# One 8-wide gather ring, 512 expert picks: fewer picks handed out beside the selection of experts, more beside attention and the routing's query products

## The chip, the cores and the metric

The kernel runs on 1 core of one Trainium2 chip. The metric is the device time of one execution in microseconds; lower is better. TensorE is called PE, VectorE DVE, ScalarE ACT, GpSimd POOL and SyncE SP.

## The reference, cut to what matters

Sequence 256, width 1024, f32. A first block of two layers, each a mixer (attention) and then a feed-forward that retrieves single-neuron experts; then a second block with four kinds of attention, gates and a dense feed-forward. The part that matters here is the retrieval. Each token takes 16 experts for each of 8 heads, 128 experts in all, out of 16384:

```python
q = (xc @ w_q).reshape(t, PEER_HEADS, 2, PEER_QDIM // 2)
sc = jnp.einsum('thpc,hpnc->thpn', q, sub_keys)
v_half, i_half = lax.top_k(sc, PEER_TOPK_HALF)
cand = (v_half[:, :, 0, :, None] + v_half[:, :, 1, None, :]).reshape(t, PEER_HEADS, -1)
top_s, pos = lax.top_k(cand, PEER_TOPK)
expert = jnp.take_along_axis(cand_idx, pos, axis=-1)
g = jax.nn.softmax(top_s, axis=-1)
act = jax.nn.gelu(jnp.einsum('thkd,td->thk', u_tab[expert], xc))
return jnp.einsum('thk,thkd->td', (g * act), v_tab[expert])
```

## The kernel before

Tokens lie in two tiles of 128 (one token per partition). For each layer and tile, `route` multiplies the queries on PE (the query products, L1361, which stream 8 MB of `in_peer_w_q`), scores them against the keys (L1350), and lets DVE take the top 16 of each list and work out the 128 expert numbers (the selection, L1414 to L1490).

After that there are 128 **picks** for this layer and tile, one for each of a token's 128 experts. A pick is: POOL gathers one row for each token (L2690: u and v rows side by side, 8 KB for each of 128 partitions) into one of 8 slots of a ring (`RING`); DVE takes the dot product of u with the token (L1532); ACT applies gelu and the share (L1548, L1549); and v times the weight is added to the output, either on PE with a diagonal matrix made by ACT (L1557, L1568) or on DVE (L1540). The addition frees the slot, and POOL can gather the next row into it. POOL takes the rows strictly in order.

The picks of one layer and tile are a **feed**. Four feeds (0: layer 0 tile 0; 1: layer 0 tile 1; 2: layer 1 tile 0; 3: layer 1 tile 1) run beside the work that comes next in the program: feed 0 beside the mixer and the routing of layer 0 tile 1, feeds 1 and 2 beside the mixer and routing of layer 1, feed 3 beside the start of the second block. Where that work may be interrupted stands a **point** with a weight. Picks are handed out in proportion to the weight passed:

```python
def handed_out(f, weight):
    return f["first"] + int(weight * min((P - HELD_BACK - f["first"]) / max(f["weight"], 1.0), RATE))
```

So 122 of 128 picks are spread over the sum of a feed's weights (at most 0.6 per unit of weight), and the last 6 come in `finish_experts`. A weight is a share, not a time: raising some points takes picks from all others. At a point every engine runs its part of the same picks, in program order with its other work. Which engine adds is set in `share_out` by the kind of point: `"dve"` points (the selection's are these) have the adding done by PE, `"pe"` points (the query products) by DVE, and at `"both"` points (attention) DVE adds every third pick and PE the others. All engines run in order, so what stands behind a waiting pick waits with it. Weights for the dense products come through a second ring of 4 slots of 1 MB, loaded by SP.

Of the kernel before, what the change touches and what calls it, by code (L numbers as in the profile page):

```python
# [144 lines left out]
def build(nc, a, out):  # L145
    with ExitStack() as ctx:
# [104 lines left out]
        def handed_out(f, weight):  # L251


            return f["first"] + int(weight * min((P - HELD_BACK - f["first"]) / max(f["weight"], 1.0), RATE))

        def point(us, filled="dve"):


            f = feeds[-1] if feeds and feeds[-1]["open"] else None
            if f is None:  # L260
                return lambda name, e: None
            f["weight"] += us
            behind = f["weight"]
            f["cuts"].append(behind)
            f["filled"].append(filled)

            def run(name, e):
                at = f["cuts"].index(behind)
                for i in range(handed_out(f, f["cuts"][at - 1] if at else 0), handed_out(f, behind)):
                    f[name](e, i)  # L270
            return run
# [438 lines left out]
        def attend(groups, maps_in=scores, beside=lambda n: None, busy=None):  # L710
# [4 lines left out]
            plan = []  # L715
# [3 lines left out]
            for g in groups:  # L719
                n_out = {"joint": 1, "diff": 2}.get(g["kind"], len(g["maps"]))  # L720
                n_turned = 2 if g["kind"] == "diff" else len(g["maps"])
                chunks = g["tile"] + 1
                apart.append(beside(len(plan)))
                if plan:
                    plan[-1]["out"] = products.take()
                value = {"s": maps_in.take(), "turns": [turns.take() for _ in range(chunks)],
                         "n_out": n_out, "n_turned": n_turned, "chunks": chunks, "w": P * chunks,
                         "m": maxes_ready.plan(), "p": probs_ready.plan()}
                if g["kind"] == "stick":
                    value["m2"] = maxes_ready.plan()  # L730
                    value["a1"] = from_act.plan()
                if g["kind"] == "diff":
                    value["a2"] = from_act.plan()
                plan.append(g | value | {"points": [point(6.0, "both"), point(6.0, "both")]})
            plan[-1]["out"] = products.take()

            def sums_of(n):
# [520 lines left out]
        def hybrid(t, score_banks, angles=None):  # L1258
# [21 lines left out]
            for j in range(2):  # L1280
# [4 lines left out]
                    values=[(lambda c, i=i: values[:, c, HD + i * HD:HD + (i + 1) * HD]) for i in hs],  # L1285
                    out_ap=mixed[:, t, 512 + 256 * j:768 + 256 * j].rearrange("p (n d) -> p n d", d=HD)))
            attend(groups, score_banks, busy=None if t else hT[:, 0:4, 0:P])
            turn_wide(M, mixedT, DC, tiles)
            project(mixedT, a["hyb_w_out"], DC, D, add_residual, "dve", tiles)
# [31 lines left out]
        def route(layer, t, beside=None, halved=False):  # L1321
# [4 lines left out]
            plan, key_units = [], []  # L1326
# [10 lines left out]
            other = beside() if beside else None  # L1337
            e_in, e_out = to_act.plan(), from_act.plan()
            routed[layer, t] = [experts_ready.plan() for _ in lots]
            made = [point(7.0, "pe") for _ in range(4)] + [point(7.0, "pe")]  # L1340
            ranked = [point(us) for us in [6.0] + 5 * [3.5] + [6.0] + 6 * [4.5]]

            def pe(e):
                def score(b):
# [757 lines left out]
        def attend_second(t, banks, tmp, bias, cum, beside=lambda n: None):  # L2102
# [41 lines left out]
            if t:  # L2144

                groups.insert(3, groups.pop(1))
            attend(groups, banks, beside)

        def diff_norm_parts(t):
# [46 lines left out]
        diff_act, diff_dve, diff_point, _ = diff_norm_parts(0)  # L2196
# [43 lines left out]
        diff_act, diff_dve, _, heads_made = diff_norm_parts(1)  # L2240
        turn_pe, turn_act, turn_dve, turn_units = turn_split_parts(H, m_pair, [(0, 0), (0, 1), (1, 0), (1, 1)])
        plan = []
# [512 lines left out]
```

## Time and profile before

| | |
|---|---|
| median of 3 runs | 2141.29 us (2138.33 to 2141.95) |
| the profiled execution | 2140.08 us, its span 2138.3 us |
| busy in the span | PE 78%, DVE 70%, ACT 37%, POOL 30% |
| moved by DMA | 744.77 MB, mean 348 GB/s |
| of it by the gathers (q0) | 536.90 MB in 512 gathers |
| the chain that ended last | PE 41%, DMA 22%, DVE 19%, ACT 9% |

Stretches are named in us from the start of the span, as the trace counts them. The line with GB/s tells in which of 40 slices the DMA moved as much as it ever does here; in the slices that don't, something else set the pace. A share of busy time over the whole span says little, since stages have different limits.

### The profile page before, as it was taken

To read this page: it belongs to the slowest core of one execution; us is meant where nothing else is said; L and a number is where in the kernel's file an instruction comes from. 1 tells how busy PE (TensorE), PEld (TensorE's weight loads), DVE (VectorE), ACT (ScalarE), POOL (GpSimd) and SP (SyncE) were. 2 spreads that over 40 slices of the span, in tenths; PEclk is the share of its full clock that TensorE was granted. 3 is DMA by queue.
4 is the path that set the end of the run, shared out by engine and by line. 5 is a ranking of instruction groups with operands and counts; after the bars stand their busy time and mean duration, and the time that the engine had idled before them with its cause. 6 is when DMAs were issued, how large, how long until landed. Compare 5 with 4: busy or idle time off the path is not lost.

```text
span 2138.3 us, 20663 instructions
## 1 busy us (share of the span) xinstructions
PE 1665.0 (78%) x6490; PEld 1000.6 (47%) x6490; DVE 1493.1 (70%) x3129; ACT 788.5 (37%) x2050; POOL 648.8 (30%) x524
## 2 busy tenths in 40 slices
PE   8797777667767865877778477765767899999998
PEld 4573343622323343333344432554333375668986
DVE  5378776897766678976666897768777455566654
ACT  1213452234424422432352235212555353444432
POOL 0013454344433443543244354335454000000000
PEclk9999899889888987998889799977888999999999
DMA  7358999999999999999999999999999775574442
GB/s 277 142 221 337 404 403 421 419 416 422 419 421 392 403 421 399 412 419 421 403 368 419 392 387 421 421 422 421 376 407 403 314 307 203 199 290 158 177 178 98
DMA packets 105515, 744.77 MB, mean 348 GB/s; under 512 B 12864, under 2 KB 13504, under 8 KB 16576
## 3 DMA queue, kind: packets, MB, share of 16 engines
q0 software_dynamic: 73728, 536.90, 61.4%
q1 hardware_dynamic: 31248, 204.98, 24.5%
q10 hardware_dynamic: 432, 1.57, 0.2%
q8 instruction: 53, 0.87, 0.2%
q14 instruction: 54, 0.44, 0.1%
HBM read 742.37 MB, written 1.05 MB: 348 GB/s over the span
## 4 chain that ended last, share of the span: by engine, by line
PE 41%; DMA 22%; DVE 19%; ACT 9%; issue 6%; DVEq 1%; POOL 1%; PEldq 1%; PEld 0%; ACTq 0%; SPq 0%; POOLq 0%
DMA sb_work<-in_peer_uv,sb_expert 19%; PE ps_acc L1568 12%; PE bank L494 6%; DVE sb_x L1540 4%; DVE sb_work L1532 4%; PE bank L1361 4%; PE bank L2056 2%; DMA sb_wring<-in_peer_w_q 2%; ACT L1548 2%; PE bank L564 2%; PE bank L565 2%; PE bank L566 2%; PE ps_acc L566 2%; PE ps_acc L564 2%; PE ps_acc L565 2%
## 5 line engine op out<-in xcount | busy, mean ns | idle before, releaser
L2690 POOL DMA_INDIRECT sb_work<-in_peer_uv,sb_expert x512 | 645.8, 1261 | 1013.3 <-PE ps_acc L1568 457.5
L1568 PE MATMUL ps_acc<-sb_work,sb_diag 128*128 128x512 f32 x1304 | 689.4, 675 | 305.1 <-ACT sb_diag L1557 261.5
L1532 DVE CUSTOM_DVE_ANT_0 sb_work<-sb_work,sb_h 128x1024 f32<-128x1024 f32 x512 | 619.8, 1223 | 189.9 <-DMA sb_work<-in_peer_uv,sb_expert 183.4
L1568 PEld LDWEIGHTS ps_acc<-sb_work,sb_diag 128*128 128x128 f32 x1304 | 264.2, 215 | 674.8 <-issue 665.5
L1548 ACT ACTIVATE sb_dots<-sb_dots 128x1 f32<-128x1 f32 x512 | 102.6, 200 | 526.6 <-DVE sb_dots L1532 497.2
L1540 DVE SCALAR_TENSOR_TENSOR sb_x<-sb_work,sb_weight,sb_x 128x1024 f32<-128x1024 f32 x186 | 238.5, 1282 | 79.6 <-ACT sb_weight L1549 79.6
L558 DVE TENSOR_TENSOR sb_work_r<-sb_wring,sb_work_r 128x2048 fp32r<-128x2048 f32 (+1 forms) x74 | 133.8, 1829 | 100.9 <-ACT sb_work_r L551 100.2
L1549 ACT ACTIVATE sb_weight<-sb_dots,sb_share 128x1 f32<-128x1 f32 x512 | 151.4, 296 | 16.7
L551 ACT CAST sb_work_r<-sb_wring 128x2048 fp32r<-128x2048 f32 (+1 forms) x74 | 112.0, 1538 | 109.7 <-PE ps_acc L566 39.1
L1361 PE MATMUL bank<-sb_hT,sb_wring 128*128 128x128 f32 x1024 | 126.8, 289 | 24.2 <-DMA sb_wring<-in_peer_w_q 21.6
L1361 PEld LDWEIGHTS bank<-sb_hT,sb_wring 128*128 128x128 f32 x1024 | 124.9, 205 | 27.7 <-issue 26.4
L1557 ACT ACTIVATE sb_diag<-sb_ident,sb_weight 128x128 f32<-128x128 f32 x326 | 131.3, 403 | 10.6
L494 PE MATMUL bank<-sb_wring,sb_hT 128*128 128x512 f32 (+2 forms) x264 | 103.4, 549 | 19.8 <-DVEq L287 14.1
L1817 PE MATMUL bank<-sb_hT,sb_wring 128*128 128x128 f32 (+1 forms) x448 | 59.5, 300 | 32.3 <-issue 24.3
L494 PEld LDWEIGHTS bank<-sb_wring,sb_hT 128*128 128x128 f32 x264 | 48.6, 199 | 75.9 <-issue 71.4
L1817 PEld LDWEIGHTS bank<-sb_hT,sb_wring 128*128 128x128 f32 (+1 forms) x448 | 58.3, 197 | 34.2 <-issue 34.2
L565 PE MATMUL ps_acc<-sb_work_r 128*128 128x256 f32 (+1 forms) x224 | 73.6, 328 | 0.0
L565 PE MATMUL bank<-sb_work_r 128*128 128x256 f32 (+1 forms) x192 | 61.1, 318 | 0.0
L494 PE MATMUL bank<-sb_work,sb_hT 128*128 128x512 f32 x128 | 58.2, 613 | 1.8 <-issue 0.9
L2056 PE MATMUL bank<-sb_wring,sb_hT 128*128 128x512 f32 x128 | 56.9, 598 | 1.5 <-DVEq L287 1.5
L494 PE MATMUL bank<-sb_wring,sb_work 128*128 128x512 f32 x128 | 55.9, 595 | 2.0 <-DVEq L287 1.2
L1385 ACT COPY sb_work<-bank 128x512 f32<-128x512 f32 x16 | 9.4, 587 | 123.5 <-PE bank L1361 123.5
(357 smaller groups left out, 2172.3 us busy)
## 6 DMA issues: line engine op xcount, KB each, us to landing
sb_wring<-in_w_mix SPq DMA_DIRECT2D x36, 1024.0 KB, 10.8
sb_wring<-in_peer_w_q SPq DMA_DIRECT2D x32, 1024.0 KB, 12.6
sb_wring<-in_w_gate SPq DMA_DIRECT2D x32, 1024.0 KB, 5.0
sb_wring<-in_w_up SPq DMA_DIRECT2D x16, 1024.0 KB, 4.8
sb_wring<-in_w_down SPq DMA_DIRECT2D x16, 1024.0 KB, 4.9
sb_wring<-in_mla_w_uq SPq DMA_DIRECT2D x12, 768.0 KB, 11.2
sb_work<-in_hyb_w_in SPq DMA_DIRECT2D x8, 1024.0 KB, 15.3
sb_wring<-in_hyb_w_out SPq DMA_DIRECT2D x8, 1024.0 KB, 8.5
```

The costliest lines, as they stand in the source:

```text
L494: last = e.matmul(u.ap[:, 0:bn], xT[:, k0 + k, t * P:(t + 1) * P], sl[:, k, b0:b0 + bn], start=k0 + k == 0, stop=k0 + k == chunks - 1)
L558: e.tensor_tensor(low, slot_ap(s)[:, k0:k0 + chunks, c0:c1], high, ALU.subtract).then_inc(lo_made.sem, 1)
L565: pe.matmul(ps, left[0], right[1], start=False, stop=False)
L1361: last = e.matmul(u.ap[:, j * P:(j + 1) * P], slot_ap(s)[:, k, j * P:(j + 1) * P], hT[:, k0 + k, t * P:(t + 1) * P], start=k0 + k == 0, st ...
L1532: e.tensor_tensor_reduce(u, u, h[:, t, :], 1.0, 0.0, ALU.mult, ALU.add, dots[:, i:i + 1]).then_inc(dot_ready, 1)
L1540: e.scalar_tensor_tensor(x[:, t, :], ring[:, n % RING, D:2 * D], weight[:, k:k + 1], x[:, t, :], ALU.mult, ALU.add).then_inc(slot_free[n % ...
L1548: link(e.activation(dots[:, k:k + 1], dots[:, k:k + 1], ACT.Gelu))
L1549: scaled = e.activation(weight[:, k:k + 1], dots[:, k:k + 1], ACT.Copy, scale=share[:, t, k:k + 1])
L1557: e.activation(diag[:, number % DIAGS, :], ident[:, :], ACT.Copy, scale=weight[:, k:k + 1]).then_inc(diag_ready, 1)
L1568: last = e.matmul(ps_acc[:, b * 512:(b + 1) * 512], diag[:, number % DIAGS, :], ring[:, n % RING, D + b * 512:D + (b + 1) * 512], start=k ...
L1817: last = e.matmul(u.ap[0:width, at:at + P], slot_ap(s)[:, k, c:c + width], hT[:, k0 + k, 0:P], start=k0 + k == 0, stop=k0 + k == DC - 1)
L2690: pool.indirect_dma_start(ring[:, n % RING, :], None, a["peer_uv"], bass.IndirectOffsetOnAxis(ap=expert[:, t, n % P:n % P + 1], axis=0)).t ...
```

## The change

Three lists of weights. In `attend` each of two points per group goes from 6.0 to 7.5; in `route` the first four points of the query products from 7.0 to 9.0 (the fifth stays at 7.0), and the 13 points of the selection from 56.5 in sum to 38.5. No pick is added or removed: picks change place among the other work, and some change the engine that adds.

```diff
@@ attend
-                plan.append(g | value | {"points": [point(6.0, "both"), point(6.0, "both")]})
+                plan.append(g | value | {"points": [point(7.5, "both"), point(7.5, "both")]})
@@ route
-            made = [point(7.0, "pe") for _ in range(4)] + [point(7.0, "pe")]
-            ranked = [point(us) for us in [6.0] + 5 * [3.5] + [6.0] + 6 * [4.5]]
+            made = [point(9.0, "pe") for _ in range(4)] + [point(7.0, "pe")]
+            ranked = [point(us) for us in [4.0] + 5 * [2.5] + [4.0] + 6 * [3.0]]
```

Counted by `handed_out` with the weights of each feed (237.4 before and 239.4 after for feed 0; 268.4 and 270.4 for feeds 1 and 2; 235.0 and 259.0 for feed 3), the picks move like this:

| beside | feed 0 | feeds 1 and 2, each | feed 3 |
|---|---|---|---|
| attention | 25 to 31 | 22 to 26 | 49 to 56 |
| query products | 18 to 22 | 16 to 19 | none |
| selection | 29 to 20 | 25 to 17 | none |
| `project_first` | none | none | 42 to 38 |
| added by DVE, whole feed | 34 to 40 | 47 to 51 | 58 to 57 |

The program of PE at the attention beside feed 0 shows the first of these. `ps_scores` are the scores, `ps_turn` the turned probabilities, `bank` the values' sums; two matmuls of L1568 add one pick (the trace has four records for them):

```order
 L752 MATMUL ps_scores<-sb_work 128x256 x8
-L1568 MATMUL ps_acc<-sb_work,sb_diag 128x512 x8
+L1568 MATMUL ps_acc<-sb_work,sb_diag 128x512 x10
 L761 MATMUL ps_turn<-sb_ident,sb_probs 128x128 x8
 L752 MATMUL ps_scores<-sb_work 128x256 x4
-L1568 MATMUL ps_acc<-sb_work,sb_diag 128x512 x4
+L1568 MATMUL ps_acc<-sb_work,sb_diag 128x512 x6
 L775 MATMUL bank<-sb_work,sb_probsT 128x64 x8
```

One pick more stands between the first scores and the turning of the probabilities, and one more before the values are summed.

On DVE, in the selection beside feed 0, the one-hot steps (L1480 compares, L1483 multiplies) have a point between them; L1532 is a pick's dot product, in two records:

```order
 L1532 ISA sb_dots 128x1
-L1532 ISA sb_work,sb_dots<-sb_work,sb_h 128x1024
-L1532 ISA sb_dots 128x1
 L1480 TENSOR_TENSOR sb_work<-sb_probsT,sb_iota 128x2048
 L1532 ISA sb_work,sb_dots<-sb_work,sb_h 128x1024
 L1532 ISA sb_dots 128x1
-L1532 ISA sb_work,sb_dots<-sb_work,sb_h 128x1024
-L1532 ISA sb_dots 128x1
 L1483 TENSOR_TENSOR sb_work<-sb_work,sb_probsT 128x2048
```

Each of these two points hands out one pick fewer, the one after L1480 one where there were two.

## Rows read from the trace of the kernel before

**Rows 1.** The page: what the DMA moved in 40 slices of 53.5 us

```profile
GB/s 277 142 221 337 404 403 421 419 416 422 419 421 392 403 421 399 412 419 421 403 368 419 392 387 421 421 422 421 376 407 403 314 307 203 199 290 158 177 178 98
```

**Rows 2.** Busy time by stretch, from the first gathered row to the last

```profile
core 0: us, PE busy (x) PEld busy (x) DVE busy (x) ACT busy (x) POOL busy (x), PEclk, DMA share, GB/s
178.60:1677.10 1498.50, 1080.35 (x3664) 577.47 (x3664) 1126.74 (x2324) 564.72 (x1705) 639.76 (x507) 0.87 0.99 406
```

**Rows 3.** The page: the queue of the gathers (packets, MB, share of 16 engines)

```profile
q0 software_dynamic: 73728, 536.90, 61.4%
```

**Rows 4.** Busy time by stretch: attention beside feeds 0, 1, 2, 3

```profile
255.60:322.60 67.00, 49.19 (x182) 26.31 (x181) 50.84 (x82) 40.29 (x117) 31.22 (x25) 0.85 0.98 393
669.60:726.70 57.10, 41.52 (x126) 21.30 (x125) 42.09 (x74) 34.52 (x105) 26.66 (x22) 0.82 0.95 378
1056.90:1120.70 63.80, 49.42 (x173) 28.32 (x173) 45.34 (x74) 38.20 (x109) 26.89 (x22) 0.81 0.94 362
1519.40:1647.00 127.60, 90.92 (x245) 43.96 (x246) 100.77 (x199) 71.81 (x195) 62.67 (x49) 0.83 0.98 391
```

**Rows 5.** Busy time by stretch: query products beside feeds 0, 1, 2

```profile
374.70:446.60 71.90, 39.83 (x286) 36.03 (x284) 63.45 (x184) 13.92 (x48) 28.31 (x20) 0.76 1.01 420
774.30:844.30 70.00, 40.85 (x293) 36.52 (x292) 58.71 (x178) 12.80 (x44) 26.01 (x19) 0.78 1.01 418
1164.80:1234.00 69.20, 39.92 (x291) 35.58 (x289) 58.83 (x178) 12.79 (x44) 25.96 (x18) 0.80 0.97 395
```

**Rows 6.** Busy time by stretch: selection beside feeds 0, 1, 2

```profile
446.60:513.50 66.90, 52.62 (x112) 20.85 (x112) 60.48 (x151) 27.72 (x87) 32.22 (x28) 0.97 1.01 418
844.30:902.10 57.80, 48.49 (x96) 19.75 (x96) 55.59 (x144) 24.11 (x75) 30.39 (x24) 0.88 0.97 394
1234.00:1291.20 57.20, 45.94 (x96) 18.35 (x96) 55.49 (x144) 24.10 (x75) 32.41 (x27) 0.94 0.97 392
```

**Rows 7.** Groups of 669.6:726.7, attention of feed 1 (busy, mean ns | idle before, releaser)

```profile
L1568 PE MATMUL ps_acc<-sb_work,sb_diag 128*128 128x512 f32 x58 | 35.2, 754 | 14.9 <-ACT sb_diag L1557 14.9
...
L1532 DVE CUSTOM_DVE_ANT_0 sb_work<-sb_work,sb_h 128x1024 f32<-128x1024 f32 x22 | 25.9, 1220 | 0.0
...
L1540 DVE SCALAR_TENSOR_TENSOR sb_x<-sb_work,sb_weight,sb_x 128x1024 f32<-128x1024 f32 x8 | 10.3, 1284 | 12.3 <-ACT sb_weight L1549 12.3
```

**Rows 8.** Busy time by stretch: inside attention, feeds 0 and 1

```profile
260.20:272.70 12.50, 11.77 (x33) 5.82 (x34) 9.77 (x16) 6.43 (x18) 6.61 (x6) 0.80 0.85 316
279.20:311.60 32.40, 22.82 (x88) 12.41 (x87) 25.49 (x40) 20.08 (x57) 14.58 (x12) 0.86 1.01 422
689.60:718.30 28.70, 21.43 (x62) 10.93 (x61) 21.78 (x40) 18.26 (x54) 13.60 (x11) 0.80 1.01 422
```

**Rows 9.** Groups of 1519.4:1647.0, attention of feed 3

```profile
L1568 PE MATMUL ps_acc<-sb_work,sb_diag 128*128 128x512 f32 x133 | 80.0, 755 | 33.8 <-ACT sb_diag L1557 33.8
...
L1532 DVE CUSTOM_DVE_ANT_0 sb_work<-sb_work,sb_h 128x1024 f32<-128x1024 f32 x50 | 60.7, 1224 | 16.7 <-DMA sb_work<-in_peer_uv,sb_expert 16.5
```

**Rows 10.** Groups of 844.3:902.1, selection of feed 1

```profile
L1568 PE MATMUL ps_acc<-sb_work,sb_diag 128*128 128x512 f32 x96 | 48.5, 663 | 10.4 <-ACT sb_diag L1557 10.3
L2690 POOL DMA_INDIRECT sb_work<-in_peer_uv,sb_expert x24 | 31.2, 1300 | 27.7 <-PE ps_acc L1568 24.8 <-issue 2.9
L1532 DVE CUSTOM_DVE_ANT_0 sb_work<-sb_work,sb_h 128x1024 f32<-128x1024 f32 x25 | 29.9, 1223 | 1.3 <-DMA sb_work<-in_peer_uv,sb_expert 0.9
```

**Rows 11.** The same group of 446.6:513.5, selection of feed 0

```profile
L1532 DVE CUSTOM_DVE_ANT_0 sb_work<-sb_work,sb_h 128x1024 f32<-128x1024 f32 x29 | 35.1, 1224 | 5.3 <-DMA sb_work<-in_peer_uv,sb_expert 4.8
```

**Rows 12.** TensorE and GpSimd around 844, selection of feed 1, in order of time

```profile
836.28 6.50 PE L1568 MATMUL ps_acc<-sb_work,sb_diag 128*128 128x512 f32 x8 [20.35 <-ACT sb_diag L1557]
...
843.05 0.94 POOL L2690 DMA_INDIRECT sb_work<-in_peer_uv,sb_expert  x1 [1.81 <-PE ps_acc L1568]
850.66 1.15 POOL L2690 DMA_INDIRECT sb_work<-in_peer_uv,sb_expert  x1 [6.67 <-PE ps_acc L1568]
```

**Rows 13.** Busy time by stretch: project_first beside feed 3

```profile
1353.40:1497.80 144.40, 88.02 (x547) 76.94 (x548) 101.75 (x126) 27.18 (x104) 60.71 (x42) 0.81 1.01 421
```

## The prediction

> **What bounds the kernel now.** I read first the page's line of what the DMA moved [rows 1]. From the fifth slice to the thirty-first it is near 400, half of the slices stand at 419 to 422, and none above. So 421 GB/s is what this core's DMA gives here, and between the first and the last gathered row the kernel is a transfer with other work beside it. The 512 gathers moved 536.90 MB [rows 3], 1.049 MB each, so one row costs 1.049 / 0.421 = 2.49 us of the DMA.
>
> The useful question is then where the DMA idled. The stretch with picks is 1498.5 us long at 406 GB/s [rows 2]: 1498.5 x (1 - 406/421) = 53 us lost. The same sum for stages (I cut them at the first dot product of each stage's picks) says where. Attention [rows 4]: 67.0 us at 393, 57.1 at 378, 63.8 at 362 and 127.6 at 391 lose 4.5, 5.8, 8.9 and 9.1 us, together 28.3. Query products [rows 5]: 0.2, 0.5, 4.3. Selection [rows 6]: 0.5, 3.7, 3.9, together 8.1. `project_first` loses nothing (421 in [rows 13]). The rest, about 12 us, is the ring's first filling and small stages. Bytes don't change, so the change is worth the difference in these losses and nothing else: a stage that merely gets longer because it consumes more rows at 421 GB/s is paid for by another that gets shorter.
>
> **When a moved pick pays.** A pick that leaves a stage where the DMA sets the pace, for another such stage, gives nothing. In a stage that an engine paces, an added pick costs c us of that engine, while it lets the DMA do 2.49 us of its work: the loss there shrinks by 2.49 - c. A pick taken from such a stage makes its loss grow by 2.49 - c.
>
> **Attention, 6 + 4 + 4 + 7 picks more.** In feed 1 DVE never waits for a row (22 dot products of 1.22 us, idle 0.0 before them [rows 7]); what it and PE wait for is ACT and each other (L1568 14.9 us for the diagonal, L1540 12.3 us for the weight). The engines pace it. Per pick, DVE pays 1.22 + 1.28/3 = 1.65 us; PE pays 35.2 us for 58 records, 14.5 picks, so 2.43 us for each that it adds, on two picks of three: 1.62 us. If both overlap, c = 1.65 and a pick is worth 0.84 us. If the two come one behind the other, c = 3.27 and each pick costs 0.78. I take 0.84: DVE is busy 42.1 and PE 41.5 of 57.1 us [rows 4], sums over 57.1, so they overlap. The stage's own evidence is that feed 0, with 25 picks in 67.0 us, loses half of what feed 2 does with 22 in 63.8.
>
> - Feeds 1 and 2: 4 x 0.84 = 3.4 us each, of 5.8 and 8.9.
> - Feed 3: 7 x 0.84 = 5.9, but half of this stage already waits for rows (16.7 us before dot products [rows 9]), where nothing is to be had. I take 4.0.
> - Feed 0: its middle is at 422 already; 3.1 us are lost in one hole of 12.5 us at 316 GB/s near the start [rows 8]. Feed 1 too has a middle at 422. Extra picks help only at holes, so of 6 x 0.84 = 5.0 I take 2.0.
>
> Sum 12.8 us. Bounds: nothing (the holes stay as they are) and 26 (all but 2 us of the 28.3).
>
> **Query products, 4 + 3 + 3 more.** DVE adds these, so one costs 1.22 + 1.28 = 2.50 us of DVE, against 2.49 of DMA. Feed 0 and 1 stand at 420 and 418 [rows 5] with DVE busy 63.5 of 71.9 and 58.7 of 70.0: room for the 10 and 7.5 us that the stage's rows themselves take. Zero.
>
> **Selection, 9 + 8 + 8 fewer.** Here DVE is the engine: 55.6 of 57.8 us [rows 6], with only 1.3 us of waits for rows [rows 10]. Without 8 picks feed 1 takes 57.8 - 8 x 1.22 = 48.0 us. Its 17 rows want 17 x 2.49 = 42.3 us. At most 5.7 us are lost, against 3.7 now. Rows still on their way when the stage starts lower that: before, 24 gathers were issued [rows 10] while 57.8 x 394 = 22.8 MB, 21.7 rows, came in, so 2.3 rows more were outstanding at the end than at the start; after, DVE is slower than the DMA and the ring need not run behind. With that whole the loss is 0, with none 5.7. At the start of this stage little is outstanding (no gather issued from 843.05 to 850.66 [rows 12]), so I take 4.7, 1.0 more than now; likewise 1.0 in feed 2. In feed 0 DVE waits 5.3 us for rows [rows 11], so it takes 66.9 - 5.3 - 9 x 1.22 = 50.6 us where 20 rows want 49.8; the picks come unevenly, 1 or 2 per point, so again 1.0. Sum +3.0 us, bounds -6 (the 8.1 nearly gone) and +6.
>
> **`project_first`, 4 fewer,** is paced by the DMA; it gets 10 us shorter, attention 7 rows longer. Zero. The cover is that PE has only 88.0 us of work in 144.4 [rows 13].
>
> **Sum:** 2140.1 (the profiled execution) - 12.8 + 3.0 = 2130.3. The median of the runs shown is 1.2 us above that execution, so 2131.
>
> **A rule weighed.** The DMA's ceiling is, by [rows 1], 422 GB/s in slices of 53 us. The Trainium skill (DMA: Bandwidth & Descriptors, Where 436 GB/s comes from) puts the port ceiling at 435 GB/s. By that a row would want 2.41 us, a pick moved to attention would be worth 0.76 and the four terms 11.6 instead of 12.8, and 1498.5 us at 406 would hold 100 us of loss. Thirteen slices that stop at the same 419 to 422 say that it can't be had here; the sum goes by 421.
>
> **Rivals.**
>
> *No change: the holes stay.* The attention losses are made by the start of the group pipeline and its end, where an engine waits for another while the ring is full, and not by too few picks; the middles of feeds 0 and 1 stand at 422 [rows 8]. For it: just that. Against it: a pick handed out ahead of a hole frees one more slot in it. Attention then gives some 3 us, selection takes 3: 2141, range 2137 to 2145.
>
> *Slower: PE falls to its lower clock in the thinned selection.* Ahead of the selection PE stands idle for 20.35 us and then needs 6.50 us for two picks, 3.25 each [rows 12], where the selection's mean is 48.5/24 = 2.02 [rows 10]; the slots are held and no gather is issued for 6.67 us. That is where feed 1's 3.7 us go. After the change PE has 17 x 2.02 = 34 us of these picks in 48.0, where it had 48.5 in 57.8, so more gaps. If the clock falls once more per selection, each costs another 3.7: 11 us. Attention's picks would have to give nothing for this to decide: 2141 + 3 + 11 = 2155 then, about 2150 with a part of the gain. It decides from one additional fall per selection on. Against it: picks that PE adds at 3.25 us still keep up with 2.8 us of DVE per pick for a while, and PE is busier in attention, where it now falls too (0.81 to 0.85 granted [rows 4]). The Trainium skill speaks for this rival (TensorE: Matmul & The Clock Gate, HAM oscillation): gaps between matmuls put the array back to the half rate, and the next burst starts slow. The row with 3.25 us per pick agrees.
>
> *Much faster: holes close.* If the added picks refill all four attentions and the query products of feed 2, 28.3 + 4.3 less some 8 are gained: 2141 - 24 = 2117.
>
> **How the numbers follow.** Runs of this kernel differ by some 0.2%, 4 us, so within 2137 to 2145.6 counts as the same. My forecast (2123 to 2137) gets 0.52, no change 0.23, slower 0.16, much faster 0.09. The forecast's own range widened to most of the second and part of the third gives 2119 to 2147. Faster: 0.52 less a little that ends above 2137, with 0.09: 0.59. Same 0.25, slower 0.16.
>
> **What would show it.** Attention at 400 GB/s or more in feeds 1 and 2 (before 378 and 362) with DVE waiting for rows in it, and some 65 and 70 us long; selection near 48 us in feeds 1 and 2 and 51 in feed 0 with DVE waits for rows gone, at 380 to 400 GB/s; query products still at 418 or more in feeds 0 and 1, some 8 us longer; the mean over the stretch with picks at 408.5 or more. Wrong if attention's rate doesn't rise, if the granted clock in selection falls below 0.85, or if stages that I left out start to lose: the first stages of a feed, which so far come with the ring behind, could find it full.

## The result and the profile after

The changed kernel takes 2152.4 us, median of 4 runs (2150.82 to 2157.0), against 2140.53 of the kernel before on the same chip (4 runs). The ratio is 1.0053, 95% interval 1.0037 to 1.007: slower by half a per cent and clear of the noise, where I had forecast 2131. The profiled execution took 2150.82 us, its span is 2149.1, so 10.8 us longer than before.

The line with GB/s of the page, as [rows 1]:

```profile
GB/s 271 146 227 336 408 416 421 418 386 403 419 421 408 412 421 415 366 388 421 417 368 395 419 375 369 421 421 421 366 422 421 323 309 210 196 293 152 178 180 98
```

The ceiling is still 421 to 422: no slice stands above. Now the stretches of the kernel after, in the form of [rows 2]. The first is the whole stretch with picks; then attention beside feeds 0 to 3 [rows 4], selection beside 0 to 2 [rows 6], two stretches that I had not cut out before (below), `project_first` [rows 13] and the query products of feeds 0 to 2 [rows 5]:

```profile
core 0: us, PE busy (x) PEld busy (x) DVE busy (x) ACT busy (x) POOL busy (x), PEclk, DMA share, GB/s
178.40:1688.80 1510.40, 1058.44 (x3612) 570.37 (x3612) 1141.94 (x2337) 559.13 (x1692) 632.71 (x507) 0.86 0.99 403
255.70:332.50 76.80, 57.16 (x198) 30.51 (x197) 60.70 (x95) 45.13 (x133) 37.68 (x31) 0.84 1.00 412
671.30:737.40 66.10, 46.80 (x138) 23.90 (x138) 49.36 (x84) 37.66 (x116) 31.17 (x26) 0.85 0.99 402
1065.90:1140.60 74.70, 57.97 (x186) 32.62 (x186) 51.94 (x83) 41.10 (x120) 30.97 (x26) 0.80 0.95 374
1518.60:1659.20 140.60, 96.80 (x265) 45.90 (x266) 112.66 (x215) 77.15 (x213) 69.94 (x56) 0.84 0.98 402
471.00:522.30 51.30, 38.96 (x76) 15.20 (x76) 49.37 (x133) 19.53 (x60) 21.90 (x19) 0.90 0.95 382
866.60:913.90 47.30, 32.53 (x64) 12.36 (x64) 46.05 (x128) 16.85 (x51) 19.76 (x16) 0.93 0.95 367
1262.70:1310.10 47.40, 32.45 (x64) 12.27 (x64) 46.15 (x128) 16.85 (x51) 21.69 (x19) 0.93 0.93 367
915.40:934.00 18.60, 17.10 (x36) 7.31 (x36) 12.06 (x22) 8.56 (x26) 9.23 (x8) 0.91 0.88 351
1311.60:1330.00 18.40, 16.90 (x36) 7.31 (x36) 11.99 (x21) 8.50 (x26) 9.34 (x8) 0.92 0.85 339
1368.50:1500.10 131.60, 85.66 (x545) 76.49 (x546) 91.88 (x117) 24.40 (x93) 58.07 (x39) 0.84 1.01 421
385.10:471.00 85.90, 41.17 (x287) 36.52 (x285) 73.09 (x195) 15.98 (x56) 32.20 (x24) 0.74 1.01 413
790.10:866.60 76.50, 41.36 (x296) 37.14 (x296) 65.92 (x187) 14.38 (x50) 29.71 (x22) 0.75 1.00 412
1188.00:1262.70 74.70, 39.98 (x288) 35.54 (x286) 65.75 (x187) 14.58 (x50) 29.34 (x21) 0.77 0.99 404
```

Time that the DMA lost is us x (1 - GB/s / 421), as in the prediction. The whole stretch ran at 403 GB/s (408.5 or more forecast) and lost 64.6 us, 11 more than before, which is the 10.8 of the span. By stage:

| | before | after | predicted | measured |
|---|---|---|---|---|
| attention, feeds 0 to 3 | 28.3 | 1.6 + 3.0 + 8.3 + 6.3 = 19.2 | -12.8 | -9.1 |
| query products | 5.0 | 1.6 + 1.6 + 3.0 = 6.2 | 0 | +1.2 |
| selection | 8.1 | 4.8 + 6.1 + 6.1 = 17.0 | +3.0 | +8.9 |
| the two stretches behind it | 0 | 3.1 + 3.6 = 6.7 | not in the sum | +6.7 |

The four rows add up to +7.7; some 3 us more lie in small stages that I left out, 2.0 of them between attention and query products of feed 2.

**The selection.** It takes as long as worked out (47.3, 47.4 and 51.3 us against 48, 48 and 51), with DVE busy nearly all of it, and the DMA falls to 367. The groups of the kernel after in 866.6:913.9, as [rows 10]:

```profile
L1568 PE MATMUL ps_acc<-sb_work,sb_diag 128*128 128x512 f32 x64 | 32.5, 650 | 14.6 <-ACT sb_diag L1557 14.6
L1532 DVE CUSTOM_DVE_ANT_0 sb_work<-sb_work,sb_h 128x1024 f32<-128x1024 f32 x17 | 20.6, 1228 | 0.5
L2690 POOL DMA_INDIRECT sb_work<-in_peer_uv,sb_expert x16 | 19.8, 1235 | 27.5 <-PE ps_acc L1568 27.5
```

DVE hardly waits for a row (0.5 us in the whole stage). POOL waits for PE's addition, PE for ACT's diagonal, and that for DVE's dot product, which stands behind the selection's own work. In order of time, DVE of the kernel after in the one-hot steps:

```profile
896.84 2.27 DVE L1486 TENSOR_REDUCE sb_probsT<-sb_work 128x128 f32<-128x2048 f32 x1
899.15 1.23 DVE L1532 CUSTOM_DVE_ANT_0 sb_work<-sb_work,sb_h 128x1024 f32<-128x1024 f32 x1
...
900.32 2.28 DVE L1480 TENSOR_TENSOR sb_work<-sb_probsT,sb_iota 128x2048 f32<-128x2048 f32 x1
902.63 1.23 DVE L1532 CUSTOM_DVE_ANT_0 sb_work<-sb_work,sb_h 128x1024 f32<-128x1024 f32 x1
```

One dot product each 3.48 us, where the DMA brings a row in 2.49. Over the stage before, it was 57.8 / 25 = 2.31 us per pick (25 dot products, 24 gathers issued [rows 10]), faster than the DMA; now 47.3 / 17 = 2.78, slower. And 16 gathers were issued while 47.3 x 367 = 17.4 MB, 16.5 rows, came in; before it was 24 against 21.7.

How many rows are on their way can be counted. When the selection of feed 1 ends, all 256 gathers of feeds 0 and 1 have been issued in both kernels. What the gathers' queue had moved until then (packets, MB), first before (0:902.1), then after (0:913.9):

```profile
q0 software_dynamic: 36162, 263.39, 71.1%
q0 software_dynamic: 36568, 266.35, 71.4%
```

At 536.90 / 512 = 1.0486 MB a row that is 251.2 and 254.0 rows: 4.8 were on their way before, 2.0 after. Counted in the same way, both kernels enter the stage with 2.5. DVE had started 249 dot products, so after the change 5.0 rows lie in the ring and wait for it, where 2.2 did.

**Behind the selection.** The six picks held back are handed out where the two tiles' streams meet; I call this place the seam. POOL of the kernel after there (start, duration, what; in brackets the wait before):

```profile
907.23 0.94 POOL L2690 DMA_INDIRECT sb_work<-in_peer_uv,sb_expert  x1 [2.53 <-PE ps_acc L1568]
910.72 0.94 POOL L2690 DMA_INDIRECT sb_work<-in_peer_uv,sb_expert  x1 [2.55 <-PE ps_acc L1568]
912.44 1.03 POOL L2690 DMA_INDIRECT sb_work<-in_peer_uv,sb_expert  x1 [0.78 <-PE ps_acc L1568]
919.80 1.12 POOL L2690 DMA_INDIRECT sb_work<-in_peer_uv,sb_expert  x1 [6.33 <-PE ps_acc L1568]
```

PE's burst of additions (this view ends at 928, the burst goes on to 931.0), and the row that DVE then waits for, in the timelines of the kernel after:

```profile
915.42 13.05 PE L1568 MATMUL ps_acc<-sb_work,sb_diag 128*128 128x512 f32 x26 [3.25 <-ACTq L287]
...
925.55 1.23 DVE L1532 CUSTOM_DVE_ANT_0 sb_work<-sb_work,sb_h 128x1024 f32<-128x1024 f32 x1 [3.15 <-DMA sb_work<-in_peer_uv,sb_expert]
```

What the DMA of the kernel after moved meanwhile, in 40 slices of 905:930:

```profile
GB/s 406 341 380 341 341 367 393 367 288 236 354 419 419 406 288 301 393 380 367 406 419 419 315 118 26 26 118 131 301 406 433 420 419 406 406 406 406 393 419 446
```

From 912.44 to 919.80, 7.36 us, nothing is issued. The 2.0 rows on their way at 913.9 are 5.0 us of work for the DMA, so they are in at about 919, and it runs dry: 26 GB/s. The same place of the kernel before, 18.6 us by windows:

```profile
903.70:922.30 18.60, 14.86 (x32) 5.57 (x32) 9.69 (x15) 7.19 (x24) 8.56 (x8) 1.00 1.01 422
```

And one row of its DVE there; the next ones are like it:

```profile
911.29 1.23 DVE L1532 CUSTOM_DVE_ANT_0 sb_work<-sb_work,sb_h 128x1024 f32<-128x1024 f32 x1 [1.26 <-DMA sb_work<-in_peer_uv,sb_expert]
```

Before, rows come every 2.49 us and are waited for. POOL pauses there too, for 4.41 us (gathers at 901.96 and 906.37), but 4.8 rows on their way are 12 us of work for the DMA, which covers it.

### The profile page after: what moved, and what is told of

Same layout as the page of the kernel before. It is cut to its first block, busy times and chain, and to the rows that moved or that the text cites. A ratio compares the mean times of both kernels' runs of the same rounds, so it can differ in the third digit from the quotient of the medians.

```text
span 2149.1 us, 20546 instructions
## 1 busy us (share of the span) xinstructions
PE 1641.6 (76%) x6438; PEld 991.3 (46%) x6438; DVE 1508.2 (70%) x3142; ACT 782.4 (36%) x2037; POOL 641.8 (30%) x524
## 3 DMA queue, kind: packets, MB, share of 16 engines
q0 software_dynamic: 73728, 536.90, 61.2%
## 4 chain that ended last, share of the span: by engine, by line
PE 38%; DMA 25%; DVE 20%; ACT 8%; issue 7%; POOL 1%; DVEq 1%; PEldq 0%; ACTq 0%; PEld 0%; SPq 0%; POOLq 0%
DMA sb_work<-in_peer_uv,sb_expert 23%; PE ps_acc L1568 11%; PE bank L494 6%; DVE sb_x L1540 4%; DVE sb_work L1532 3%; PE bank L1361 3%; PE bank L2056 2%; PE bank L564 2%; PE ps_acc L564 2%; PE ps_acc L566 2%; PE ps_acc L565 2%; PE bank L565 1%; PE bank L566 1%; ACT L1548 1%; PE bank L775 1%
## 5 line engine op out<-in xcount | busy, mean ns | idle before, releaser
L2690 POOL DMA_INDIRECT sb_work<-in_peer_uv,sb_expert x512 | 637.7, 1245 | 1030.8 <-PE ps_acc L1568 438.4
L1568 PE MATMUL ps_acc<-sb_work,sb_diag 128*128 128x512 f32 x1252 | 667.2, 680 | 339.5 <-ACT sb_diag L1557 264.0
L1532 DVE CUSTOM_DVE_ANT_0 sb_work<-sb_work,sb_h 128x1024 f32<-128x1024 f32 x512 | 620.7, 1223 | 214.1 <-DMA sb_work<-in_peer_uv,sb_expert 203.4
L1568 PEld LDWEIGHTS ps_acc<-sb_work,sb_diag 128*128 128x128 f32 x1252 | 256.4, 217 | 696.9 <-issue 685.4
L1540 DVE SCALAR_TENSOR_TENSOR sb_x<-sb_work,sb_weight,sb_x 128x1024 f32<-128x1024 f32 x199 | 254.9, 1281 | 51.3 <-ACT sb_weight L1549 51.1
L1557 ACT ACTIVATE sb_diag<-sb_ident,sb_weight 128x128 f32<-128x128 f32 x313 | 125.7, 401 | 13.8 <-PE ps_acc L1568 3.8
L494 PE MATMUL bank<-sb_wring,sb_hT 128*128 128x512 f32 (+2 forms) x264 | 99.3, 532 | 12.9 <-DVEq L287 7.4
L1817 PEld LDWEIGHTS bank<-sb_hT,sb_wring 128*128 128x128 f32 (+1 forms) x448 | 58.6, 199 | 27.4 <-issue 27.3
L752 PE MATMUL ps_scores<-sb_work 64*128 64x128 f32 (+5 forms) x196 | 33.7, 371 | 29.2 <-DVE sb_probs L885 14.8
```

The costliest lines, as they stand in the source:

```text
L494: last = e.matmul(u.ap[:, 0:bn], xT[:, k0 + k, t * P:(t + 1) * P], sl[:, k, b0:b0 + bn], start=k0 + k == 0, stop=k0 + k == chunks - 1)
L1532: e.tensor_tensor_reduce(u, u, h[:, t, :], 1.0, 0.0, ALU.mult, ALU.add, dots[:, i:i + 1]).then_inc(dot_ready, 1)
L1540: e.scalar_tensor_tensor(x[:, t, :], ring[:, n % RING, D:2 * D], weight[:, k:k + 1], x[:, t, :], ALU.mult, ALU.add).then_inc(slot_free[n % ...
L1557: e.activation(diag[:, number % DIAGS, :], ident[:, :], ACT.Copy, scale=weight[:, k:k + 1]).then_inc(diag_ready, 1)
L1568: last = e.matmul(ps_acc[:, b * 512:(b + 1) * 512], diag[:, number % DIAGS, :], ring[:, n % RING, D + b * 512:D + (b + 1) * 512], start=k ...
L1817: last = e.matmul(u.ap[0:width, at:at + P], slot_ap(s)[:, k, c:c + width], hT[:, k0 + k, 0:P], start=k0 + k == 0, stop=k0 + k == DC - 1)
```

## The experiments

The profiled executions are compared by the DMA's lost time in all feeds. This table takes each stretch's MB at 0.4215 MB per us, so it differs from the sums above by tenths; "seam" goes from the first of the picks held back to the first pick at a point of the next feed; "all" is the whole stretch with picks. What "all" holds beyond the four columns before it, the ring's first filling and small stages, is 11.7 us before, 15.3 after and 14.6 to 24.2 in the other runs. The differences of the totals agree with those of the spans to within 3 us in every run. A row shows one execution, which can lie some us off the median: `att_only` was profiled at 2138.5, `att_thin_end` at 2135.75. Ratios are to the kernel before, run in between on the same chip.

| run | median us | ratio (95%) | attention | query | selection | seam | all |
|---|---|---|---|---|---|---|---|
| before | | 1 | 28.7 | 5.0 | 8.3 | 0.0 | 53.7 |
| after | 2152.40 | 1.0053 (1.0037 to 1.007) | 19.8 | 6.6 | 17.0 | 7.3 | 66.0 |
| att_only | 2132.71 | 0.9961 (0.9947 to 0.9976) | 20.2 | 6.2 | 7.7 | -0.1 | 54.1 |
| qry_only | 2143.48 | 1.0016 (1.0006 to 1.0027) | 22.9 | 6.5 | 10.0 | 0.2 | 58.0 |
| sel_only | 2150.09 | 1.0048 (1.0034 to 1.0061) | 28.5 | 3.3 | 11.5 | 8.2 | 67.2 |
| after_sel_back | 2134.24 | 0.9973 (0.9962 to 0.9984) | 24.1 | 2.3 | 9.5 | 0.2 | 51.0 |
| after_warm | 2154.73 | 1.0064 (1.0051 to 1.0077) | 20.8 | 7.7 | 18.4 | 6.7 | 69.9 |
| after_late | 2162.37 | 1.0098 (1.0083 to 1.0114) | 21.6 | 8.9 | 34.0 | 1.6 | 82.2 |
| att_thin_end | 2138.67 | 0.9986 (0.9975 to 0.9998) | 16.3 | 7.4 | 8.2 | 4.1 | 52.0 |
| att9 | 2133.16 | 0.9959 (0.9945 to 0.9972) | 12.9 | 11.9 | 9.0 | 0.2 | 48.6 |
| att_thick | 2148.21 | 1.0031 (1.0016 to 1.0045) | 35.0 | 6.6 | 6.6 | 0.0 | 64.6 |
| att_thick_turn | 2135.05 | 0.9968 (0.9955 to 0.998) | 14.8 | 8.5 | 7.3 | 0.1 | 50.6 |
| before_short | 2157.33 | 1.0082 (1.0068 to 1.0097) | 27.3 | 7.4 | 9.8 | 0.2 | 65.5 |
| after_short | 2162.38 | 1.0101 (1.0088 to 1.0115) | 27.7 | 10.3 | 17.6 | 0.2 | 80.0 |

The diffs below are to the kernel before, if nothing else is said.

### One list at a time

`att_only`, attention's weights alone:

```diff
-                plan.append(g | value | {"points": [point(6.0, "both"), point(6.0, "both")]})
+                plan.append(g | value | {"points": [point(7.5, "both"), point(7.5, "both")]})
```

> Only the attention's points are raised to 7.5; query products and selection keep their weights, so beside feeds 1 and 2 the picks are 26 in attention, 15 in the query products and 24 in the selection (before 22, 16, 25; after 26, 19, 17), and feed 3 is as in the changed kernel. Theory A (the thinned selection costs, attention gains): attention loses 9 us less of DMA time than before, selection stays at about 8 lost and no hole opens behind it: 2140.5 - 9 = 2131 to 2134. Rival B (picks in attention are what costs, by pushing feed 3 and the stages behind attention): 2148 or more.

0.9961. The profiled execution is its slowest, 2138.5 us. Attention beside feeds 1 and 2, selection beside feed 1 and the stretch behind it:

```profile
663.10:728.20 65.10, 48.97 (x142) 24.62 (x141) 48.10 (x83) 37.90 (x116) 32.95 (x26) 0.84 0.99 404
1050.70:1122.40 71.70, 57.46 (x190) 32.97 (x189) 50.94 (x83) 41.35 (x120) 29.99 (x26) 0.86 0.96 383
...
843.10:899.10 56.00, 45.02 (x92) 17.84 (x92) 54.27 (x143) 23.18 (x72) 27.53 (x23) 0.94 0.97 397
900.60:919.10 18.50, 14.78 (x32) 5.63 (x32) 10.14 (x17) 7.19 (x24) 8.78 (x8) 1.00 1.01 422
```

With this list alone the kernel is faster, by about what was expected, and a selection with 24 picks leaves the seam at 422. The trace shows only a part of it: in the profiled execution attention loses 8.5 us less than before, but the small stages lose 20.1 where they lost 11.7, so its total is no lower.

`qry_only`, the query products' four points alone:

```diff
-            made = [point(7.0, "pe") for _ in range(4)] + [point(7.0, "pe")]
+            made = [point(9.0, "pe") for _ in range(4)] + [point(7.0, "pe")]
```

> Only the first four points of the query products go to 9.0: 19 picks there for 16 beside feeds 1 and 2, attention 21 for 22, selection 24 for 25; feed 3 is as before. Theory A: the query products are paced by the DMA and cost 1.5 us, attention loses 1 to 2 more: 2142 to 2144. Rival C (picks whose sum is made by DVE in the query products delay the scores' top 16 and are the main cost): 2148 or more.

1.0016: small, on the costly side, as expected. What lies behind it is not as expected. The query products lose 1.5 us more and the selection 1.7, but attention, which has one pick fewer in each of feeds 1 and 2, loses 22.9 instead of 28.7, and not 1 to 2 more. Attention beside feed 1, with 21 picks for 22 and 417 GB/s for 378:

```profile
670.60:725.30 54.70, 37.84 (x126) 20.28 (x126) 40.51 (x72) 33.70 (x102) 23.13 (x21) 0.91 1.01 417
```

`sel_only`, the selection's weights alone:

```diff
-            ranked = [point(us) for us in [6.0] + 5 * [3.5] + [6.0] + 6 * [4.5]]
+            ranked = [point(us) for us in [4.0] + 5 * [2.5] + [4.0] + 6 * [3.0]]
```

> Only the selection's points are thinned (sum 38.5 for 56.5): beside feeds 1 and 2 it gets 18 picks for 25, attention 23, query products 17; feed 3 is as before. Theory A: the selection's loss goes from 8 to about 16 us and 7 us of hole open at the seam between selection and the next stage, attention gains 2: 2151 to 2155. Rival B: selection costs 1 to 3 us only: 2141 to 2143.

1.0048: nearly the whole of the change's result, at the seam above all (8.2 us). The selections lose 11.5, 3.2 more than before, where about 16 had been expected. Selection beside feeds 1 and 2, and the stretch behind the first:

```profile
860.70:909.10 48.40, 35.81 (x68) 13.85 (x68) 47.17 (x130) 17.74 (x54) 20.24 (x17) 0.89 0.97 387
1260.10:1308.60 48.50, 35.79 (x68) 13.85 (x68) 47.23 (x131) 17.82 (x54) 22.35 (x20) 0.89 0.94 370
910.70:929.00 18.30, 16.96 (x32) 7.01 (x32) 10.77 (x18) 6.96 (x24) 9.15 (x8) 0.83 0.88 335
```

The seam is as dry as in the kernel after (335 against 351).

The three lists don't add up. By themselves they make -0.39%, +0.16% and +0.48%, in sum +0.25%; together they make +0.53%. The first two together (`after_sel_back`, next) are -0.27%, near their sum, so it is the thinned selection that costs more beside the other two than alone. Its stages lose 17.0 us there against 11.5; why was not tried.

`after_sel_back` is the kernel after with the selection's old weights:

> The changed kernel with the selection's old weights (sum 56.5): beside feeds 1 and 2 attention 25, query products 18, selection 23 picks. Theory A: the selection's loss goes from 17 to 9 us and the seam closes (7 to 0), attention keeps its gain: 2133 to 2138. Rival (the sum of small shifts costs, not the selection): 2145 or more.

0.9973, by the ratios 0.8% or some 17 us below the change as a whole. Selection beside feed 1, and the stretch behind it:

```profile
850.10:904.90 54.80, 43.99 (x88) 17.52 (x88) 53.04 (x142) 22.27 (x69) 28.14 (x22) 0.91 0.97 392
...
906.40:925.00 18.60, 14.68 (x32) 5.72 (x32) 10.85 (x18) 7.18 (x24) 8.73 (x8) 1.00 1.01 421
```

Both the selection and the seam recover when this list alone is put back.

### Is it TensorE's clock?

`after_warm` adds matmuls that nobody reads to the kernel after:

```diff
-                for p in made[4:] + ranked:
+                if not halved:
+                    for _ in range(20):
+                        e.matmul(ps_turn[0][:, :], ident[:, :], h[:, 1 - t, 0:512], start=True, stop=True)
+                for p in made[4:]:
                     p("pe", e)
+                for p in ranked:
+                    p("pe", e)
+                    if not halved:
+                        e.matmul(ps_turn[0][:, :], ident[:, :], h[:, 1 - t, 0:512], start=True, stop=True)
```

> The changed kernel, with matmuls that nobody reads on PE: 20 behind the last score product of a routing and one behind each point of the selection, so that PE doesn't stand idle ahead of and in the selection. The work that counts is the same. Rival D (PE's lower clock holds the slots in the thinned selection): the granted clock there goes to 1.0 and the time to 2140 or less. Theory A (DVE paces the selection, and the ring is full at its end): only the slow picks at its start get quicker, at most 2 to 3 us in each of three selections: 2144 to 2152.

1.0064, no faster. Selection beside feeds 0 and 1:

```profile
468.00:519.40 51.40, 46.37 (x100) 18.93 (x100) 49.47 (x133) 19.57 (x60) 22.05 (x19) 0.97 0.95 385
867.40:914.80 47.40, 40.89 (x88) 16.80 (x88) 46.16 (x128) 16.84 (x51) 18.02 (x16) 0.96 0.96 362
```

The granted clock rose from 0.90 to 0.97 in feed 0 and from 0.93 to 0.96 in feed 1, not to the 1.0 that rival D had said, and the stages lost as much as without the extra matmuls (385 GB/s against 382, 362 against 367). The added matmuls are themselves work for PE, so this run alone would not exclude a small effect. In the kernel after, the change had moved the clock of the three selections from 0.97, 0.88 and 0.94 [rows 6] to 0.90, 0.93 and 0.93: lower in feed 0, higher in feed 1. One matmul record of an addition in feed 1 took 650 ns on average, against 663 [rows 10].

### Where in the selection the picks stand

`after_late`: the kernel after, with the selection's weight moved to its second half (3 picks in the first six points, 14 in the last seven):

```diff
-            ranked = [point(us) for us in [4.0] + 5 * [2.5] + [4.0] + 6 * [3.0]]
+            ranked = [point(us) for us in [1.0] + 5 * [1.0] + [5.5] + 6 * [4.5]]
```

> The changed kernel with as many picks in each selection (20, 17, 17), but placed late: beside feeds 1 and 2 the 13 points hand out 3 picks in the first six and 14 in the last seven (changed kernel: 7 and 10). Theory A1 (a part of the loss is the hole at the seam behind the selection, which opens because DVE paces its last points and no rows are left outstanding): the rate in the 18 to 21 us behind the selection goes back from 350 to 400 GB/s or more, and the time falls by 3 to 7 us against the changed kernel: 2145 to 2149. Rival (the number of picks in the selection is all that counts, not where in it they stand): 2150 to 2155, with the seam as it was.

1.0098, a miss: 13 us above the range. The seam closed for the most part (1.6 us, from 7.3), but the selection lost 34.0. Selection beside feed 1, and four microseconds near its start:

```profile
878.10:924.00 45.90, 33.44 (x64) 12.33 (x64) 44.22 (x116) 16.86 (x51) 17.74 (x16) 0.89 0.87 338
...
882.60:886.60 4.00, 3.24 (x4) 0.92 (x4) 3.91 (x27) 0.90 (x3) 0.94 (x1) 0.50 0.22 43
```

A ring that is full is not fed, and no later pick makes up for it: 43 GB/s over 4 us is 3.6 us gone at once. I had counted only the seam.

`att_thin_end`: attention at 7.5, and the selection with as many picks as `att_only` (24 in feeds 1 and 2) but 6 of them in its last six points:

```diff
-            ranked = [point(us) for us in [6.0] + 5 * [3.5] + [6.0] + 6 * [4.5]]
+            ranked = [point(us) for us in [8.0] + 5 * [5.0] + [8.0] + 6 * [2.5]]
```

> The kernel with only attention raised, and in the selection as many picks as there (27, 24, 24), but placed early: 18 in the first seven points and 6, one each, in the last six. Theory A1: DVE paces the last six points at 3.4 us a pick, the ring fills, the seam behind opens (some 350 to 400 GB/s there instead of 421) and 3 to 7 us are lost against the kernel with attention alone (2132.7): 2135 to 2140. Rival (only the number counts): 2131 to 2134.

0.9986, by the medians 6 us above `att_only`. The stretches behind the selections of feeds 1 and 2:

```profile
906.80:925.40 18.60, 17.12 (x36) 7.18 (x36) 12.31 (x22) 8.66 (x26) 7.91 (x8) 0.91 1.01 410
1297.40:1316.00 18.60, 17.12 (x36) 7.26 (x36) 12.35 (x22) 8.79 (x27) 9.54 (x8) 0.92 0.92 370
```

With the number of picks unchanged, thinning the last six points is enough to open the seam (4.1 us in all: 1.2, 0.5 and 2.3 by feed).

### Is it only DVE's own work in the selection?

`before_short` and `after_short` leave out the second round of one-hot steps in each kernel (half of the expert number is set to 0, so other rows are gathered):

```diff
+                        if s:
+                            link(e.tensor_scalar(found, where, 0.0, None, ALU.mult))
+                            for _ in range(3):
+                                take_point()
+                            break
```

> The kernel before, with a part left out: the second of the two one-hot rounds of each selection (compare, multiply, reduce over 128x2048, 6.8 us of DVE) is replaced by a zero, so the second half of an expert's number is 0 and other rows are gathered; their count and size are the same. Theory A: 7 us saved ahead of the first feed, where nothing hides it, and the selections beside feeds lose 2 to 4 us instead of 8: 2127 to 2131. Rival (DVE doesn't pace the selection): 7 us saved alone, 2133 to 2134.

> The changed kernel with the same part left out. Theory A (DVE paces the thinned selection and empties what is outstanding behind it): each of three selections gets some 7 us shorter with its rows hardly slower, its loss goes from 17 to 4 to 8 in sum, and the seam closes by half or more: 2129 to 2136, and the distance to before_short is 8 us or less instead of 12. Rival: only the 7 us ahead of the first feed are saved: 2144 to 2146, distance 12.

Both slower than expected, 2157.33 and 2162.38. The whole stretch, and selection beside feed 1, of `before_short`:

```profile
178.40:1688.00 1509.60, 1086.99 (x3663) 582.13 (x3664) 1108.31 (x2317) 564.17 (x1705) 619.74 (x507) 0.86 1.00 403
853.10:911.70 58.60, 48.79 (x96) 19.73 (x96) 49.23 (x142) 24.06 (x75) 28.06 (x24) 0.88 0.99 393
```

DVE had 6 us less to do in it, and the stage takes 0.8 us longer. Other rows are gathered, so this pair compares only with itself. Within it the change costs 5 us by the medians instead of 12 (the profiled executions are 10.9 apart), and the seam is closed in both. Attention gained nothing in this pair: 27.3 and 27.7 us. But selection beside feed 1 of `after_short` still loses 7.1 us, though DVE now needs 41.5 / 17 = 2.44 us per pick:

```profile
876.30:917.80 41.50, 34.17 (x64) 13.81 (x64) 39.42 (x127) 16.89 (x51) 19.72 (x15) 0.84 0.94 349
```

The three selections of `after_short` lose 17.6 us, where 4 to 8 had been expected. So DVE's mean pace accounts for the seam, and not for all that the selection loses; how the picks lie in it counts too, as `after_late` shows.

### More for attention

`att9`: attention at 9.0 and a heavier selection, so that it keeps 26 picks:

```diff
-                plan.append(g | value | {"points": [point(6.0, "both"), point(6.0, "both")]})
+                plan.append(g | value | {"points": [point(9.0, "both"), point(9.0, "both")]})
-            ranked = [point(us) for us in [6.0] + 5 * [3.5] + [6.0] + 6 * [4.5]]
+            ranked = [point(us) for us in [7.0] + 5 * [4.0] + [7.0] + 6 * [5.5]]
```

> Attention at 9.0, selection at a sum of 68: beside feeds 1 and 2 attention 29, query products 14, selection 26 picks; beside feed 3 attention 61 and project_first 35. If the gain in attention per added pick went on, another 3 us per feed: 2124 to 2128. If the holes in attention are made by waits between the engines and not by too few picks, it is spent: attention still loses 15 or more, the other stages lose more, and the time is 2131 to 2138. I hold the second likelier.

0.9959, within the likelier of the two ranges: attention down to 12.9 us (15 or more had been said), but the query products up to 11.9. No better than `att_only`.

`att_thick` has the same selection and attention at 7.5:

> Attention at 7.5, query products as before, and the selection thicker than before (sum 68 for 56.5): beside feeds 1 and 2 attention 25, query products 14, selection 28 picks. Theory A carried on: the selection is paced by the DMA, its loss goes from 8 towards 3 us and nothing opens at the seam; attention and query products lose as with attention alone: 2126 to 2131. Rival (stages that get fewer picks, norms, turns and query products, lose what the selection gains): 2132 to 2136.

1.0031, where 2126 to 2131 had been expected. The selection did as said (6.6), but attention lost 35.0 us. `att_thick_turn` is the same, with another of every three picks given to DVE:

```diff
-                    if filled == "pe" or filled == "both" and k % 3 == 2:
+                    if filled == "pe" or filled == "both" and k % 3 == 0:
```

> The kernel att_thick (thick selection, 2148.2 us) with the picks that DVE adds at attention's points shifted by one: every third pick as before, but those with number 0 modulo 3 instead of 2. In att_thick all points of attention beside feeds 1 and 2 began with DVE's pick and ended with two of PE's, only 3 or 4 rows were issued ahead behind them, and attention lost 35 us instead of 20. Theory E (the place of DVE's pick within a point sets how early slots come free): attention loses 16 to 22 and the time is 2128 to 2136. Rival (too many picks in the selection leave too few elsewhere): 2145 to 2151, unchanged.

0.9968, 13 us faster than `att_thick`. Attention beside feed 1, the window and two groups, first `att_thick`:

```profile
664.90:732.60 67.70, 47.00 (x134) 23.90 (x133) 47.95 (x81) 36.21 (x113) 27.59 (x25) 0.80 0.95 366
```

```profile
L1568 PE MATMUL ps_acc<-sb_work,sb_diag 128*128 128x512 f32 x66 | 40.4, 770 | 20.0 <-ACT sb_diag L1557 20.0
...
L2690 POOL DMA_INDIRECT sb_work<-in_peer_uv,sb_expert x25 | 27.6, 1104 | 41.6 <-PE ps_acc L1568 33.1 <-DVE sb_x L1540 4.6 <-issue 4.0
```

then `att_thick_turn`:

```profile
660.20:722.10 61.90, 46.39 (x138) 23.52 (x137) 46.28 (x80) 37.10 (x113) 32.73 (x25) 0.86 1.01 421
```

```profile
L1568 PE MATMUL ps_acc<-sb_work,sb_diag 128*128 128x512 f32 x70 | 39.7, 711 | 14.8 <-ACT sb_diag L1557 14.8
L2690 POOL DMA_INDIRECT sb_work<-in_peer_uv,sb_expert x25 | 32.7, 1309 | 30.4 <-PE ps_acc L1568 16.8 <-DVE sb_x L1540 10.6 <-issue 3.0
```

With the same 25 picks it is 366 or 421 GB/s. POOL takes slots strictly in order, and waits 33.1 or 16.8 us for PE's: which pick of a point DVE adds is as large a lever as how many there are, and every change of any weight shifts it.

## Why the prediction was wrong

**The bound was right.** 421 to 423 is the highest slice in every run, and lost DMA time accounts for the span to within 3 us each time.

**Attention: right in sign, too large, and the price per pick is not shown.** -12.8 predicted, -9.1 measured. Feeds 0, 1 and 3 gave 2.9, 2.8 and 2.8 (I took 2.0, 3.4 and 4.0). Feed 2 gave 0.6 instead of 3.4: it went from 362 to 374 GB/s only. `att_only` has 383 there with the same 26 picks, and the turned pair shows that such differences can come from which pick DVE adds; that this is the cause in feed 2 of the kernel after was not tried. DVE now waits for rows in feed 1's attention (14.6 us before its dot products, against 0.0 in [rows 7]), as I said it would. `att_only` at 0.9961 shows that the heavier list gains. It does not show that each added pick is worth 0.84 us, and beside feed 1 the runs speak against it. By the table's measure attention lost 0.6 us there with 21 picks (`qry_only`), 6.0 with 22 (before), 5.1 with 23 (`sel_only`), 0.1 or 9.0 with 25 (`att_thick_turn`, `att_thick`) and 2.9 with 26 (after). The place of DVE's pick moves the loss by more than four picks were to bring, and any weight shifts it; as a rival to the number of picks it stands for feeds 0, 1 and 2. Only in feed 3 does the loss follow the number in most runs: 9.2 us with 49 picks, 6.6 with 56, 4.0 with 61 (before, after, `att9`), 0.4 us a pick. The sum had also taken c = 1.65, as if DVE's and PE's work overlapped whole; two engines busy 42.1 and 41.5 us of 57.1 show an overlap of 26.5 us at least, and not a whole one.

**Query products: 0 predicted, +1.2 measured.** `qry_only` agrees in sign, 1.0016. Feeds 0 and 1, where I saw room for the picks, fell from 420 and 418 to 413 and 412 GB/s, below the 418 that I had named as the sign; feed 2 rose from 395 to 404. Why was not tried.

**Selection: the step that failed.** The stage's length was right to a microsecond. The loss was bounded at 48.0 - 42.3 = 5.7 us and taken at 4.7 since "rows still on their way when the stage starts lower that". They did not: feed 1 began with 2.5 rows on their way and ended with 2.0. Its 16.5 rows are 41.2 us of the DMA in 47.3 us, so it lost 6.1, and feed 2 as much. Feed 0, taken at 0.5 + 1.0, lost 4.8: 51.3 us for 20 picks is 2.57 us each, slower than the DMA as well, and 18.7 rows came in. In all +8.9 in place of +3.0, above the upper bound of 6. With the selection's list changed alone (`sel_only`) it was +3.2, so a part of the excess comes with the other two lists.

**The term that was missing: what the stage handed on.** In the same sentence I worked out that the selection before ended with 2.3 rows more on their way than it began with, and used it only to lower the loss inside it. Those rows covered the seam behind it, where POOL issues nothing for 7.4 us after the change and 4.4 before. Without them 6.7 us are lost in feeds 1 and 2. I named the place at the end, as something that could go wrong ("which so far come with the ring behind, could find it full"), and gave it no price; the rows to begin pricing it stood in the trace of before. `sel_only` (8.2 at the seam), `after_sel_back` (0.2) and `att_thin_end` (4.1 with the picks' number unchanged) show the cause. The two together, +15.6 instead of +3.0, turn the forecast of -9.8 into slower.

**The slower rival** gave nearly the right time, 2150 to 2155, by a mechanism that the runs don't bear out: the clock in the selection fell markedly in feed 0 alone (0.97 to 0.90) and nowhere below 0.85, the additions took no longer in feed 1, and raising the clock gave nothing. Its argument against itself held a slip: 3.25 us per pick on PE don't keep up with 2.8 on DVE. The Trainium skill (TensorE: Matmul & The Clock Gate, HAM oscillation) warns of gaps between matmuls; here PE was busy for 32.5 of 47.3 us in the selection of feed 1, against 48.5 of 57.8, and the granted clock went from 0.88 to 0.93.

**A threshold that fits.** DVE's own work in the selection of feed 1 is 57.8 less 1.3 us of waits and 25 x 1.22 for the dot products, 26.0 us; in the kernel after it is 47.3 - 0.5 - 17 x 1.22 = 26.1. By this estimate it keeps up with the DMA if 26.1 / n + 1.22 is below 2.49, so from n = 20.6 picks on. `after_sel_back` with 23, `att_only` with 24 and `att9` with 26 leave no loss at the seam; `sel_only` with 18 and the kernel after with 17 lose 8.2 and 7.3. Nothing between 18 and 23 was run beside feeds 1 and 2, so the runs place the threshold no more closely than that. `att_thin_end`, with 24 but few at the end, shows that it must hold for the last points too.

**Open.** Why the kernels with half of the expert number set to 0 are slower throughout; and how much of the selection's loss comes from DVE's pace and how much from how the picks lie in it, since the pair meant to tell that apart changed the rows as well; and what attention's gain owes to the number of picks and what to the place of DVE's.

## What to carry to other kernels

In a kernel bound by transfers, a stage may not only be asked what it loses but what it leaves in flight for the next one: count issues against bytes landed over the stage. Take work of a shared stream only from stages whose engine still needs less time per item than the transfer does, own work included; here the estimate is some 21 picks, and the change went to 17. And when a list of weights is retuned, measure each list by itself and all together: one of these three gains 0.4%, one loses 0.5%, and together they lose more than their sum.

## What the hardware showed that I had not expected

- The DMA's share says little about how full it is. In the selection of the kernel after it reads 0.95 at 367 GB/s, and at full rate 1.01 at 421: 6% less share, 13% less moved. The GB/s is the column to read.
- A gather issued when the DMA has run dry takes long: the one at 919.80 in the kernel after was waited for until 925.55, 5.75 us, against 2.49 per row in a stream. The Trainium skill (DMA: Bandwidth & Descriptors, Anatomy of one DMA) gives a fixed 2.0 us beside the bytes' time, from which 1.049 MB would take an estimated 4.4 us; the order of size agrees, and it is what rows in flight hide.
- With expert numbers whose second half is 0 (rows 128 apart), the kernel is slower: `before_short` has 403 GB/s over the whole stretch against 406 [rows 2], and takes 2157.33 us with less work for DVE. Its highest slice is 422 as before. The cause wasn't looked into.
